# Start addresses of the weight ring, output weights, keys and transposed probabilities in SBUF, in a hybrid attention layer

## The reference

```python
h = rms_norm(x, norm_pre_g[layer])
proj = jnp.einsum('bsd,de->bse', h, w_in[layer])
q_a, k_a, v_a, g_a, f_a, q_b, k_b, v_b, g_b = jnp.split(proj, offsets, axis=-1)
log_f = jax.nn.log_sigmoid((f_a + fox_forget_b[layer]).astype(jnp.float32))
y_a = fox_attention(q_a, k_a, v_a, log_f) * jax.nn.silu(g_a)
...
y_b = moba_attention(q_b, k_b, v_b, slopes) * jax.nn.silu(g_b)
y = jnp.einsum('bse,ed->bsd', jnp.concatenate([y_a, y_b], axis=-1), w_out[layer])
x = x + rms_norm(y, norm_post_g[layer])
```

## Time and profile before

| | |
|---|---|
| median of 3 runs | 144.2 us (143.92 to 144.43) |
| the profiled execution's time | 143.9 us |
| its span | 142.1 us |
| TensorE busy | 134.8 us (95%) |
| VectorE busy | 109.1 us (77%) |
| ScalarE busy | 96.9 us (68%) |
| GpSimd busy | 38.9 us (27%) |

### The profile page before, as it was taken

One profiled execution on the slowest core, in us unless ns is written; L12 is line 12 of the kernel. 1 busy time (PEld: TensorE's weight loads), 2 busy tenths in 40 slices (PEclk: granted clock), 3 DMA queues, 4 the chain that ended last, 5 costly groups with the idle time before them and its releaser, 6 DMA issues.

```text
span 142.1 us, 2849 instructions
## 1 busy us (share of the span) xinstructions
PE 134.8 (95%) x1074; PEld 127.6 (90%) x1074; DVE 109.1 (77%) x226; ACT 96.9 (68%) x199; POOL 38.9 (27%) x59
## 2 busy tenths in 40 slices
PE   7989999999999999999999999999999999999930
PEld 7879999999999999999999999999998888988830
DVE  0384967999999898988898995999679835561691
ACT  4377989379965478886883977788969913351860
POOL 3621100000000078000399417050565470320002
PEclk9999999999999999999999999999999999999995
DMA  3799999489765999855368704449800000000034
GB/s 107 218 346 383 405 395 350 133 344 325 243 191 173 393 406 311 318 160 178 127 214 250 261 12 152 148 148 253 342 5 0 0 0 0 5 0 0 0 148 148
DMA packets 9725, 26.96 MB, mean 190 GB/s; under 512 B 1384, under 2 KB 2416, under 8 KB 9456
## 3 DMA queue, kind: packets, MB, share of 16 engines
q1 hardware_dynamic: 9120, 25.57, 52.4%
q10 hardware_dynamic: 592, 1.22, 2.3%
HBM read 25.73 MB, written 1.06 MB: 189 GB/s over the span
## 4 chain that ended last, share of the span: by engine, by line
PE 87%; DMA 3%; DVE 3%; ACT 2%; SPq 1%; issue 1%; POOLq 1%; ACTq 0%
PE bank L950 47%; PE score_banks L960 11%; PE bank L1142 7%; PE score_banks L1142 5%; PE score_banks L1047 4%; PE value_banks L960 4%; DMA raw<-in_w_units 3%; PE value_banks L1058 1%; PE value_banks L1070 1%; PE value_banks L1074 1%; PE value_banks L1059 1%; DVE x_t L911 1%; ACT squares L603 1%; PE bank L1060 1%; DVE h L905 1%
## 5 line engine op out<-in xcount | busy, mean ns | idle before, releaser
L634 DVE TENSOR_TENSOR w_lo<-raw,w_hi 128x1024 fp32r<-128x1024 f32 (+1 forms) x33 | 44.4, 1349 | 5.6 <-ACT w_hi L388 5.5
L388 ACT ACTIVATE w_hi<-raw 128x1024 fp32r<-128x1024 f32 (+1 forms) x33 | 34.5, 1055 | 6.4 <-PE bank L950 3.2
L950 PE MATMUL bank<-h_hi,w_hi 128*128 128x256 f32 x128 | 35.8, 280 | 0.0
L950 PE MATMUL bank<-h_lo,w_hi 128*128 128x256 f32 x128 | 35.4, 276 | 0.0
L950 PE MATMUL bank<-h_hi,w_lo 128*128 128x256 f32 x128 | 35.4, 276 | 0.0
L950 PEld LDWEIGHTS bank<-h_hi,w_hi 128*128 128x128 f32 x128 | 24.0, 188 | 0.4
L950 PEld LDWEIGHTS bank<-h_lo,w_hi 128*128 128x128 f32 x128 | 24.0, 188 | 0.0
L950 PEld LDWEIGHTS bank<-h_hi,w_lo 128*128 128x128 f32 x128 | 24.0, 188 | 0.0
L344 POOL TENSOR_TENSOR probs<-probs,row_inv 128x256 f32<-128x256 f32 (+1 forms) x16 | 15.7, 1006 | 27.8 <-DVE row_inv L787 27.6
L950 PE MATMUL bank<-xg_hi,w_hi 128*128 128x256 f32 x64 | 17.9, 279 | 0.0
L950 PE MATMUL bank<-xg_lo,w_hi 128*128 128x256 f32 x64 | 17.8, 278 | 0.0
(11 more groups left out here) (173 smaller groups left out, 322.8 us busy)
## 6 DMA issues: line engine op xcount, KB each, us to landing
raw<-in_w_units SPq DMA_DIRECT2D x30, 512.0 KB, 4.9
raw<-in_w_out SPq DMA_DIRECT2D x4, 512.0 KB, 3.3
h<-in_x SPq DMA_DIRECT2D x2, 512.0 KB, 8.0
y_parts<-in_w_out SPq DMA_DIRECT2D x2, 512.0 KB, 5.9
gpost_row<-in_w_out SPq DMA_DIRECT2D x2, 512.0 KB, 5.6
squares<-decay_rows_scratch ACTq DMA_DIRECT2D x1, 1024.0 KB, 5.9
x_t<-in_x SPq DMA_DIRECT2D x1, 1024.0 KB, 7.4
raw<-in_w_units SPq DMA_DIRECT2D x3, 256.0 KB, 5.0
```

The source lines that it names most:

```text
L388: nc.scalar.activation(w[0][:, s, 0:width], raw[:, s, 0:width], ACT.Copy).then_inc(s_hi, 1)
L634: nc.vector.tensor_tensor(w[1][:, s, 0:width], raw[:, s, 0:width], w[0][:, s, 0:width].bitcast(F32), ALU.subtract).then_inc(s_lo, 1)
L950: last = nc.tensor.matmul(dst, stationary(a, j), moving(b, j), start=n == 1, stop=n == count * len(PASSES))
```

## The change

Six unused tensors are added or resized between the others, and with them the start addresses behind change. `RING_SHIFT` goes from 32 floats to 16, so the ring's w_hi and w_lo start 64 bytes lower; the unused tensors behind grow, so that v, q, probs and all that follows the last one keep their address modulo 256.

| tensor | start modulo 256, before | after |
|---|---|---|
| w_hi, w_lo, slots 0 to 3 | 64, 192, 64, 192 | 0, 128, 0, 128 |
| wo_hi, wo_lo | 192 | 128 |
| k_hi, k_lo | 192 | 128 |
| p_t0, p_t1, both parts | 192 | 128 |
| xg, h, x_t | 128 | 128 |
| raw, slots 0 to 3 | 192, 64, 192, 64 | 192, 64, 192, 64 |
| v, q, bias, probs, gate, y_parts, ident | 192 | 192 |

k also holds the two parts of a diagonal matrix (`diag`) for a short product at L1008. No instruction is added, removed or moved on any engine, and no wait or DMA.

```diff
--- before.py
+++ after.py
@@ -38,7 +38,9 @@
 V_UNITS = KT
 V_WIDTH = D_MODEL + HEADS
 V_PITCH = 1056
-RING_SHIFT = 32
+RING_SHIFT = 16
+LINE = 64
+MOVING_BACK = 16
 V_GROUPS = ((0, HALF), (HALF, HALF + SEQ), (HALF + SEQ, V_WIDTH))
 PIECES = (((0, SEQ), (SEQ, HALF), (HALF, HALF + SEQ), (HALF + SEQ, V_WIDTH)), ((0, HALF), (HALF, V_WIDTH)),
           ((0, HALF), (HALF, V_WIDTH)))
@@ -89,18 +91,24 @@
         raw = sb("raw", [P, RING, V_PITCH])
         sb("ring_shift", [P, RING_SHIFT])
         w = [sb(f"w_{n}", [P, RING, V_PITCH], F32R) for n in PARTS]
-        sb("ring_shift_back", [P, RING_SHIFT])
+        sb("ring_shift_back", [P, LINE - RING_SHIFT])
+        sb("wo_shift", [P, LINE - MOVING_BACK])
         wo = [sb(f"wo_{n}", [P, OUT_OWN, D_MODEL], F32R) for n in PARTS]
+        sb("wo_shift_back", [P, MOVING_BACK])
         v = sb("v", [P, TT, 2 * HEADS, 2, HEAD_DIM], F32R)
 
 
 
         q = [sb(f"q_{n}", [P, 4, SEQ], F32R) for n in PARTS]
+        sb("k_shift", [P, LINE - MOVING_BACK])
         k = [sb(f"k_{n}", [P, 2, SEQ], F32R) for n in PARTS]
+        sb("k_shift_back", [P, MOVING_BACK])
         bias = sb("bias", [P, 4, P])
         probs = sb("probs", [P, 4, NB])
+        sb("p_shift", [P, LINE - MOVING_BACK])
         p_t0 = [sb(f"p_t0_{n}", [P, 4, SEQ], F32R) for n in PARTS]
         p_t1 = [sb(f"p_t1_{n}", [P, 4, P], F32R) for n in PARTS]
+        sb("p_shift_back", [P, MOVING_BACK])
         gate = sb("gate", [P, PAIRS, SEQ])
         y_parts = sb("y_parts", [P, 4, SEQ])
         ident = sb("ident", [P, P])
```

## The result

The changed kernel takes **146.47 us** (median of 6 runs, 146.40 to 146.83) against 143.93 us for the kernel before beside it: ratio 1.0178, 95% interval 1.0163 to 1.0193. It is slower by 1.8%, where 143.0 us and a faster kernel were forecast. All ratios compare fast executions alone; one of experiment 2 (148.15 us) and one of experiment 9 (145.42 us) were slow and do not count in theirs. The profiled execution took 146.4 us with a span of 144.6 us.

A forecast was written before the change was run, and what follows sets the result against it. TensorE's start-to-start matmul step was taken to bound the kernel; gains of 0.44 + 0.33 + 0.38 + 0.10 = 1.25 us gave 143.0 us against a median of 144.2, range 141.8 to 145.6.

The forecast's parts named there:

- Long and short states: Gate, query and key matmuls, start to start: 99 of 576 at about 117.8 ns, 477 at 113.3, about 4.5 ns apart.
- The gates: Gate units, stationary slots moved from 64/192 to 0/128: their 99 long matmuls become short, gaining 0.44 us.
- The lower bound: Worst case of the gates term: the 477 short matmuls turn long, 2.15 us lost.
- the slower one: Rival, 25%: short step needs both operands 64 bytes apart modulo 128, which the change takes away; 145.2 us.
- its full form: Slower rival with units of all four slots losing the short step: 146.3 us.
- its half form: Slower rival with units of two of four slots losing the short step: 1.05 us on top, 145.2 us.
- The second point against it: Against the slower rival: transposes have operands 0 apart and are the fastest, 110 ns each.
- The transposes agree: Transposes' 110 ns said to match the Trainium skill's start-to-start estimate of 109.2 ns for 256 columns.
- Output projection: Moving wo mostly to 128: 63 matmuls of 512 and 24 of 256 columns gain 0.38 us before group 0 closes.
- Value stage: Moving ring slots to 0 or 128: 0.66 us at most over 150 matmuls, half taken, 0.33 us gained.
- Scores and values: 24 score and 32 value steps of 256 columns, moving k and p_t to 128: 0.10 us gained, 0.25 at most.
- No effect: Rival, 20%: the step depends on how TensorE's read streams fall into phase, not on place; 144.2 us, switch points move by chance.

The follow-up runs named there:

- experiment 2: The changed kernel with the ring's w_hi and w_lo alone back at 64 and 192 (wo, k, p_t stay at 128): 144.23 us, ratio 1.0012.
- experiment 9: The kernel before with all four w slots at 192, and k, p_t0 and p_t1 at 128: 143.78 us, ratio 0.9991.
- experiment 1: The kernel before with the ring's w_hi and w_lo alone moved to 0 and 128: 146.73 us, ratio 1.0198.
- experiment 3: The changed kernel with x_t, xg, h32, h and squares 64 bytes higher, at 192: 144.17 us, ratio 1.0011.
- experiment 4: The kernel before with x_t, xg, h32, h and squares 64 bytes higher, at 192: 146.71 us, ratio 1.0179.
- the map: Bare TensorE kernel, no layer computed: 64 pairs of moving and stationary starts, 128x256 matmuls; 113.3 ns at distance 64, up to 120.0 elsewhere.
- Experiment 8: The kernel before with all four w slots at 64 modulo 256: 146.39 us, ratio 1.0154.
- experiment 6: Bare kernel again with 128, 256, 264 and 512 columns, moving start 0 and 128, stationary 0 to 224; 512 columns: 226.7 ns at distance 0, 233.3 at 64.
- experiment 11: Bare 256-column map with each place entered without pause behind 24 matmuls at distance 64; distance 192 stayed 113.3 or 117.8 ns as entered.
- experiment 7: The kernel before with w_hi and w_lo at a pitch of 1088 floats, all four slots at 192: 143.47 us, ratio 0.9970.
- experiment 12: The kernel before with all four w slots at 192 and k alone at 128, p_t0 and p_t1 at 192: 143.46 us, ratio 0.9937.
- experiment 10: The kernel before with all four w slots at 192 and two TensorE waits on its own work, before units 8 and 12: 144.67 us, ratio 1.0025.

## Why the prediction was wrong

**The bound and the way of reading were right.** TensorE's step, read from start times and not from busy time, carries all of the change. Long and short states exist, the loss falls on L950, and VectorE and ScalarE were rightly costed at nothing.

**The step that failed is "The gates".** It set a gain of 0.44 us, "nearest to the rows where a 128-byte moving operand settles". The earlier trace rows fit two readings: the moving start at 128, or the stationary operand 64 bytes ahead of the moving one. I took the first. Experiments 1, 3 and 4 and the map show the second; the change took the distance from 192 and 64 to 128 and 0, where no run has a lasting short state, and the units lost 2.63 us. The lower bound stood in the text as 477 x 4.5 = 2.15 us; measured were 2.63 us within the units, since the new places run at 118.3 and 120.0 ns, not at 117.8, and also slow the 99 long ones. Experiment 8, with 117.8 ns everywhere, lost 1.92 us within the units. Why a distance makes the step shorter stays open.

**The rival that came true was the slower one**, in its full form: 146.3 us was written beside it, 146.47 measured, but it got 25% and its half form, 145.2. That the two times lie so close is partly luck: 146.3 stood on 144.2 us and a loss of 2.15, the measured time on 143.93 and a loss of 2.54. Its condition, 64 apart modulo 128, is refuted by experiment 8: only the stationary operand 64 above the moving one settles short by itself. Against it I held that value and output stages are 64 apart as well and long. That was a distance without its sign: there the stationary operand starts 64 bytes below the moving one, 192 modulo 256 (all of wo, half of the ring), and for 512 columns the order of distances is another anyway (experiment 6). The other half of the ring, slots 0 and 2, has the distance 64 in the value stage, and its 256-column matmuls still take about 119 ns (unit 4, from 17.60 us on); only two stand in a row between other widths there, and whether that is the reason was not tried. The second point against it was the transposes' 110 ns. They are fp32 matmuls of 128 columns, so "The transposes agree" sets them beside 109.2 ns, a value worked out for 256 columns; they say nothing for or against a distance at 256.

**The other terms.** Output projection, predicted 0.38 us: wo's 512 columns won 2 ns (229 to 227), its 256 columns lost 2 (118 to 120), and the ring's 512 columns lost 1 (230.3 to 231.6). The whole stage, from its first matmul's start to its last one's, took 26.76 us before (109.33 to 136.09) and 26.81 after (111.77 to 138.58). Here too the term took a moving start of 128 for the cause: at 128 wo ran at 120 ns with y at 128 and at 113.3 with y at 192 (experiment 3). Value stage, predicted 0.33: two units 5.64 us before, 5.66 after, nothing. Scores and values, predicted 0.10: beside the 2.63 us within the units, output, scores, values and the steps between units together come to 0.03 us more, so there is no gain either. The range ended at 145.6, below a bound that the text itself had worked out as 146.3; with two readings of the same rows and no row to tell them apart, it should have reached it.

**No effect** held for the switch points only: at distance 64 and 192 the state depends on what ran before (experiment 11), and may differ at the same places (experiments 7 and 12).

## What to carry over

Where TensorE bounds a kernel, take the start-to-start step of each form by the place of both operands; for 128x256 fp32r matmuls at 2.4 GHz here the stationary operand belongs 64 bytes above the moving one modulo 256 (113 ns against up to 120), and tensors in a ring need a pitch that keeps it for every slot. That brought 0.3% to 0.6% in experiments 7 and 12, nothing clear in experiment 9; the wrong distances cost 1.5% to 2.0% (experiments 1, 4 and 8). When a profile's rows differ in two things at once, a place and a distance, put the full loss of the other reading into the range. Measure a few places in a bare kernel before moving tensors: one run mapped 64.

## What the runs showed of the hardware that was not expected

- The step of 128x256 fp32r matmuls depends on the difference of the operands' starts modulo 256 bytes: 113.3 ns at 64, 116.7 to 120.0 elsewhere; for 512 columns 226.7 at 0, 228.8 at 192, 232.6 to 234.6 elsewhere; for 264 columns 120.0 to 125.0 with no short one.
- At differences 64 and 192 there are two lasting states, 113.3 and 117.8 ns; which one holds depends at least in part on the matmuls ahead. From rest 192 never found the short one in these runs, and 64 mostly did; behind 512-column matmuls at 192 the ring's 256-column ones ran short once (experiment 7) and long three times (9, 10 and 12).
- Bare kernels begin with 213 ns for a 256-column matmul and 330 to 333 ns for a weight load, and fall to 118 to 120 and 188 to 192 ns. In experiment 6 that fall came only behind all 16 places with 128 columns, at 135 us; 128-column matmuls among the values of the layer kernel take about 60 ns. What keeps it away was not tried.
